# First slab on its own, its transfers ahead of the others, a fourth bank for slab 3, products of zeros at the start

## What is computed

```python
def rms_norm(x, g):
    y = xf * lax.rsqrt(jnp.mean(xf * xf, axis=-1, keepdims=True) + EPS)
    return (y * g.astype(jnp.float32)).astype(x.dtype)

for l in range(DEPTH):
    h = rms_norm(x, norm_mix_g[l])
    proj = h @ w_in[l]
    pa, pb, pc, pg = jnp.split(proj, GROUP_POINTS, axis=-1)
    oa = rwkv7_time_mix(pa, ...)      # decay, a and g come from the first 256 columns of pa
    ob = stick_breaking_attention(pb)
    oc = differential_attention(pc, ...)
    merged = ga * (oa @ w_branch_a[l]) + gb * (ob @ w_branch_b[l]) + gc * (oc @ w_branch_c[l])
    x = x + merged @ w_out[l]
    x = x + conv_ffn(rms_norm(x, norm_ffn_g[l]), ...)
```

## Time and profile before

| | us |
|---|---|
| median of 3 runs | 1148.99 |
| lowest, highest | 1147.91, 1149.82 |
| the profiled execution, its own time | 1146.43 |
| its span | 1144.5 |

### The profile page before, as it was taken

One profiled execution on the slowest core, in us unless ns is written; L12 is line 12 of the kernel. 1 busy time (PEld: TensorE's weight loads), 2 busy tenths in 40 slices (PEclk: granted clock), 3 DMA queues, 4 the chain that ended last, 5 costly groups with the idle time before them and its releaser, 6 DMA issues.

```text
span 1144.5 us, 26139 instructions
## 1 busy us (share of the span) xinstructions
PE 1089.9 (95%) x10100; PEld 1029.7 (90%) x10100; DVE 832.5 (73%) x1429; ACT 595.8 (52%) x884; POOL 2.5 (0%) x8
## 2 busy tenths in 40 slices
PE   6999999899999999999999999998999999999997
PEld 6998878789889999999999888877998899999996
DVE  5598586475768788778868975946657777877886
ACT  5861221555565655555578403026565656555556
POOL 0000000000000000000000000000000000000000
PEclk9999999999999999999999999999999999999999
DMA  7352321234435465665633413122453455556553
GB/s 277 110 168 93 94 92 57 74 129 149 150 119 193 132 217 168 189 188 173 187 128 129 149 61 108 58 92 73 135 172 130 144 179 163 187 178 190 182 173 125
DMA packets 46048, 163.47 MB, mean 143 GB/s; under 512 B 5552, under 2 KB 5728, under 8 KB 45968
## 3 DMA queue, kind: packets, MB, share of 16 engines
q1 hardware_dynamic: 45072, 160.88, 43.7%
q10 hardware_dynamic: 720, 1.14, 0.3%
q0 software_dynamic: 176, 0.29, 0.1%
HBM read 161.24 MB, written 1.05 MB: 142 GB/s over the span
## 4 chain that ended last, share of the span: by engine, by line
PE 72%; DVE 16%; ACT 6%; issue 5%; DMA 1%; DVEq 0%; ACTq 0%; SPq 0%
PE psum L441 71%; DVE sb_lo L1171 4%; ACT sb_rw L839 2%; ACT sb_inv L839 2%; ACT sb_hi L839 1%; DVE sb_inv L1379 1%; DVE sb_rw L1254 1%; DVE sb_inv L1387 1%; DVE sb_yf L1401 1%; DVE sb_small L1456 1%; DMA sb_raw<-w_stream 1%; DVE sb_rw L1239 0%; DVE sb_rw L1312 0%; DVE sb_inv L1369 0%; ACT sb_rs L839 0%
## 5 line engine op out<-in xcount | busy, mean ns | idle before, releaser
L441 PE MATMUL psum<-sb_hh,sb_hi 128*128 128x256 f32 x1568 | 457.5, 292 | 19.5 <-DVE sb_hl L1178 9.5
L441 PE MATMUL psum<-sb_hl,sb_hi 128*128 128x256 f32 x1568 | 446.6, 285 | 0.0
L441 PE MATMUL psum<-sb_hh,sb_lo 128*128 128x256 f32 x1568 | 446.3, 285 | 0.0
L839 ACT ACTIVATE sb_hi<-sb_raw 128x1024 fp32r<-128x1024 f32 (+1 forms) x301 | 313.2, 1046 | 248.3 <-PE psum L441 240.5
L1171 DVE TENSOR_TENSOR sb_lo<-sb_raw,sb_hi 128x1024 fp32r<-128x1024 f32 x297 | 362.4, 1221 | 100.2 <-ACT sb_hi L839 98.2
L441 PEld LDWEIGHTS psum<-sb_hh,sb_hi 128*128 128x128 f32 x1568 | 303.4, 194 | 29.1 <-issue 23.9
L441 PEld LDWEIGHTS psum<-sb_hl,sb_hi 128*128 128x128 f32 x1568 | 303.8, 194 | 2.0 <-issue 1.9
L441 PEld LDWEIGHTS psum<-sb_hh,sb_lo 128*128 128x128 f32 x1568 | 303.6, 194 | 0.0
L441 PE MATMUL psum<-sb_oh,sb_hi 128*128 128x256 f32 x672 | 192.4, 286 | 7.9 <-DVE sb_ol L1502 4.7
L441 PE MATMUL psum<-sb_ol,sb_hi 128*128 128x256 f32 x672 | 190.1, 283 | 0.0
L441 PE MATMUL psum<-sb_oh,sb_lo 128*128 128x256 f32 x672 | 190.1, 283 | 0.0
(11 more groups left out here) (166 smaller groups left out, 1027.6 us busy)
## 6 DMA issues: line engine op xcount, KB each, us to landing
sb_raw<-w_stream SPq DMA_DIRECT2D x298, 512.0 KB, 3.8
sb_pm<-mix_par ACTq DMA_DIRECT2D x2, 512.5 KB, 3.6
sb_raw<-w_stream SPq DMA_DIRECT2D x4, 256.0 KB, 6.1
sb_x<-x_t SPq DMA_DIRECT2D x4, 256.0 KB, 6.7
y_t<-sb_rw SPq DMA_DIRECT2D x4, 256.0 KB, 2.3
sb_cf<-const_f SPq DMA_DIRECT2D x1, 739.0 KB, 8.9
sb_pm<-mix_par SPq DMA_DIRECT2D x1, 512.5 KB, 10.4
sb_pf<-ffn_par POOLq DMA_DIRECT2D x3, 92.0 KB, 2.2
```

Of the source, the lines that this page charges most:

```text
L441: return pe.matmul(out, lhsT, rhs, start=start, stop=stop, skip_group_check=True)
L839: return act.activation(out, in_, func, scale=scale, bias=bias, **kw)
```

## The change

The outputs of the dense slabs get a table of banks: m = 0 to 3 go to banks 0, 1, 2 and 5, later ones go round banks 0 to 2; output 3 waits for none, output 4 for output 0, and so on, in both layers. "up" in addition waits until output 3 has been emptied, since it writes bank 5 too. In the first layer slab 0 is done alone (`first_slab`) and slab 1 as an ordinary slab; in the second layer the two stay woven. SP's first transfers are the halves of slab 0 with x tiles 0 to 3 between and behind them, then x tiles 4 to 7 in one, slabs 1 and 2 whole. ACT and DVE split slab 0 and x first, then slabs 1 and 2 whole. POOL's two loads wait until all eight tiles of x have been split. DVE first sets a 128 x 256 piece of `XSQ` to zero, and PE multiplies it with itself five times, in fp32, into bank 7; ACT's squares wait for that.

```diff
+BANK = [0, 1, 2, 5] + [(m - 4) % 3 for m in range(4, len(OUTS))]
+BEFORE = {m: max(p for p in range(m) if BANK[p] == BANK[m]) for m in range(4, len(OUTS))}
...
+X_PART = [slice(0, 2), slice(2, 4), slice(4, 8)]
...
-                sp.dma_start(x[:, 2 * b:2 * b + 2, :], x_t[:, 2 * b:2 * b + 2, :]).then_inc(x_in[b], 16)
-            for s in range(2):
-                sp.dma_start(raw[:, s, HALF[0]], w_in[s, :, HALF[0]]).then_inc(first_in[s], 16)
-                load_x(s)
-            for s in range(2):
-                sp.dma_start(raw[:, s, HALF[1]], w_in[s, :, HALF[1]]).then_inc(raw_in[s], 16)
-                load_x(2 + s)
-            sp.dma_start(raw[:, 2], w_in[2]).then_inc(raw_in[2], 16)
+                k = X_PART[b]
+                sp.dma_start(x[:, k, :], x_t[:, k, :]).then_inc(x_in[b], 16)
+            sp.dma_start(raw[:, 0, HALF[0]], w_in[0, :, HALF[0]]).then_inc(first_in, 16)
+            load_x(0)
+            sp.dma_start(raw[:, 0, HALF[1]], w_in[0, :, HALF[1]]).then_inc(raw_in[0], 16)
+            load_x(1)
+            load_x(2)
+            for s in (1, 2):
+                sp.dma_start(raw[:, s], w_in[s]).then_inc(raw_in[s], 16)
...
+            pool.wait_ge(split_l, KT)
...
-                    if m >= 3 and (n == 0 or m not in OUT_OF[n - 1]):
-                        pe.wait_ge(*n_out(l, m - 3))
+                    if m in BEFORE and m not in OUT_OF[n - 1]:
+                        pe.wait_ge(*n_out(l, BEFORE[m]))
...
+            def first_slab():
+                pe.wait_ge(first_lo, 1)
+                for k in range(KT):
+                    if k == KT // 2:
+                        pe.wait_ge(lo_done, 1)
+                    pe.wait_ge(split_l, k + 1)
+                    cols = slice(k * P, (k + 1) * P)
+                    last = split_mm(bank[0][:, 0:T], (hi[:, 0, cols], lo[:, 0, cols]), (hh[:, k, :], hl[:, k, :]),
+                                    k == 0, k == KT - 1)
+                last.then_inc(slab_done, 1)
...
+                    pe.wait_ge(*n_out(l, 3))
...
+            pe.wait_ge(zeros_set, 1)
+            for n in range(5):
+                last = mm(bank[7][:, 0:T], XSQ[:, 0, 0:P], XSQ[:, 0, :], n == 0, n == 4)
+            last.then_inc(zeros_used, 1)
...
-                            if l == 0 and b % 2 == 0:
-                                first_hi_of(b // 2)
-                                act.wait_ge(x_in[b], 16)
+                                if b < 2:
+                                    first_hi_of(b)
+                                if b < 3:
+                                    act.wait_ge(x_in[b], 16)
-                            split(2, 2, None, 16)
+                            for n in range(1, AHEAD):
+                                split(n, n, None, 16)
+                            act.wait_ge(zeros_used, 1)
...
-                            for t in range(4 * half, 4 * half + 4):
+                            for t in range(2, KT) if half else range(2):
-                        split(2, 2, None, None)
+                        for n in range(1, AHEAD):
+                            split(n, n, None, None)
...
+            dve.memset(XSQ[:, 0, :], 0.0).then_inc(zeros_set, 1)
```

More of the change, by code:

```diff
@@ L334, in hybrid_blocks @@
         const_in, fin_loaded = sem("const_in"), sem("fin_loaded")
-        x_in = [sem(f"x_in{b}") for b in range(4)]
-        first_in = [sem(f"first_half_in{s}") for s in range(2)]
+        x_in = [sem(f"x_in{b}") for b in range(3)]
+        first_in = sem("first_half_in")
         first_hi, first_lo = sem("first_half_hi"), sem("first_half_lo")
@@ L476, in dense @@
                             k, cols = 2 * i + k2, slice(k2 * BW, (k2 + 1) * BW)
-                            last = split_mm(bank[m % 3][:, :], (hh[:, k, tok], hl[:, k, tok]),
+                            last = split_mm(bank[BANK[m]][:, :], (hh[:, k, tok], hl[:, k, tok]),
                                             (hi[:, s, cols], lo[:, s, cols]), k == 0, k == KT - 1)
@@ L483, in dense @@
                             cols = slice(k * 2 * P + u * P, k * 2 * P + (u + 1) * P)
[L484 removed]
+                            last = split_mm(bank[BANK[m]][:, u * T:(u + 1) * T], (hi[:, s, cols], lo[:, s, cols]),
                                             (oh[:, b * BT + k, :], ol[:, b * BT + k, :]), u == 0 and k == 0,
@@ L493, in dense @@
                         cols = slice(k * P, (k + 1) * P)
-                        last = split_mm(bank[m % 3][:, 0:T], (hi[:, s, cols], lo[:, s, cols]),
+                        last = split_mm(bank[BANK[m]][:, 0:T], (hi[:, s, cols], lo[:, s, cols]),
                                         (src[0][:, k, :], src[1][:, k, :]), k == 0, k == KT - 1)
@@ L500, in two_slabs @@
             def two_slabs(slab, s0_, tiles):
[L502 to L505, removed]
+                pe.wait_ge(lo_done, slab + 2)
                 for k in range(KT):
-                    if slab == 0 and k == KT // 2:
-                        pe.wait_ge(lo_done, 2)
                     pe.wait_ge(split_l, tiles + k + 1)
@@ L533, in step @@
                 if kind == "D" and s[1] == 0:
-                    two_slabs(l * SLABS, 0, l * 2 * KT)
-                elif kind == "D" and s[1] > 1:
+                    if l:
+                        two_slabs(l * SLABS, 0, l * 2 * KT)
+                    else:
+                        first_slab()
+                elif kind == "D" and (s[1] > 1 or l == 0):
                     dense(l, s[1])
@@ L870, in empty @@
                     for tt, m in enumerate(OUT_OF[n]):
-                        do((vb if kind == "Bv" else vc)[:, tt, :], bank[m % 3][:, :], ACT.Copy,
+                        do((vb if kind == "Bv" else vc)[:, tt, :], bank[BANK[m]][:, :], ACT.Copy,
                            scale=rs[:, T + tt:T + tt + 1]).then_inc(emptied["act"], 1)
@@ L1086, in first_hi_of @@
             def first_hi_of(half):
-                for s in range(2):
-                    act.wait_ge((raw_in if half else first_in)[s], 16)
-                    do(hi[:, s, HALF[half]], raw[:, s, HALF[half]], ACT.Copy).then_inc(hi_done if half else first_hi, 1)
+                act.wait_ge(raw_in[0] if half else first_in, 16)
+                do(hi[:, 0, HALF[half]], raw[:, 0, HALF[half]], ACT.Copy).then_inc(hi_done if half else first_hi, 1)
                 if half == 0:
@@ L1209, in empty @@
             def empty(l, n):
-                kind, b = DENSE[n][0], bank[OUT_OF[n][0] % 3]
+                kind, b = DENSE[n][0], bank[BANK[OUT_OF[n][0]]]
                 if n == A_SLABS:
@@ L1505, in first_lo_of @@
             def first_lo_of(half):
-                for s in range(2):
-                    if half:
-                        dve.wait_ge(hi_done, s + 1)
-                    else:
-                        dve.wait_ge(first_hi, s + 1)
-                    cols = HALF[half]
-                    tt(lo[:, s, cols], raw[:, s, cols], hi[:, s, cols].bitcast(F32), ALU.subtract)\
-                        .then_inc(lo_done if half else first_lo, 1)
+                cols = HALF[half]
+                dve.wait_ge(hi_done if half else first_hi, 1)
+                tt(lo[:, 0, cols], raw[:, 0, cols], hi[:, 0, cols].bitcast(F32), ALU.subtract)\
+                    .then_inc(lo_done if half else first_lo, 1)
             def add_down(l, b):
```

5 lines of the change are left out of this document (3 added, 2 removed).

## The result

| | us |
|---|---|
| median after, 5 runs | 1142.01 (1140.27 to 1142.97) |
| median before, 5 runs | 1147.91 (1146.06 to 1149.82) |
| ratio, 95% interval | 0.9948 (0.9931 to 0.9965) |
| profiled execution after, its own time and span | 1142.97, 1141.3 |

The change is 5.9 us faster, against 5.2 forecast (1143.8, range 1140.9 to 1147.2). The time itself is 1.8 us under the forecast one: 0.7 is gain, and 1.1 comes from the kernel before, whose median is 1147.91 here and was 1148.99 in the three runs that the forecast started from.

What follows compares the result with a forecast made beforehand. PE was busy 1089.9 of 1144.5 us, so only its idle and slow time could be won: 1.6 (start) + 1.8 + 1.8 (layers) = 5.2 us, 1148.99 to 1143.8; own range 1142.4 to 1145.2, 8-in-10 range 1140.9 to 1147.2.

Steps and rivals of the forecast that it cites:

- The start: Program start to first norm: earlier x and slab 1, PE at the upper clock level in slabs 1 and 2; 1.6 us.
- second limit: ACT's first norm operation stands behind slab 5's split: slab 5 lands at 19.9, norm from 21.0, gain 1.5 us.
- signs of being wrong: Norm-to-sigmoids distance on ACT above 13, slab 1 after 14, or PE at 0.20 us a product in slabs 1 and 2.
- The waits inside slab 0: Slab 0 waits for x; expected upper clock level anyway, though by the skill's rule the start would be worth 0.3 us.
- rival (c): PE at the lower clock level when slab 1 starts, for one stretch: 3.9 us gained, 1145.1; chance 0.06.
- The zeros: Five fp32 products ahead of slab 0, over by about 5.7, before x arrives at 6.5: cost 0.
- The bank: Slab 3 behind the norm starts without waiting for DVE; ACT's sigmoids start 1.8 us earlier in each layer.
- (a): PE's whole loss comes back, at the start and 2.7 us a layer: 7.6 us gained, 1141.4; chance 0.14.
- (b): The start gives nothing or costs, by old transfer pace and one half-clock stretch: 2.8 us gained, 1146.2; chance 0.18.
- (d): The banks give nothing because later waits of ACT and DVE absorb it: 1.6 us alone, 1147.4; chance 0.06.
- (e): Slower: PE waits for slab 1 until 14.6, lower clock level through slab 3: 2.4 us lost, 1151.4; chance 0.04.
- The disturbance is moved and not removed: By the skill's rule, delaying POOL's loads only shifts the slow transfers, leaving the start the 1.5 us of the second limit.

Runs made afterwards that it cites:

- the second profile: The changed kernel, unaltered, timed and profiled again beside the other kernels: 1140.82 us, ratio 0.9948 to the kernel before.
- the run with E 3 first: The changed kernel with DVE's emptying of slab 3's bank moved ahead of slab 6's lo part, both layers: 1140.09 us, ratio 0.9949.

## Why the prediction was right

The sign, the size and the path are right: 5.2 us forecast, 5.9 measured twice. The time, 1142.01, is in the range and just under the narrower one that was given for the forecast itself (1142.4 to 1145.2). Both layers' terms are shown. The term of the start is not, and that the whole came so near is in part luck. By its steps:

**The start, 1.6 us.** Its numbers on transfers and splits held: first product at 6.5 (6.94), all x on ACT at 10.6 (11.0), slab 1 from 12.9 (13.26), slab 5 at 19.9 (19.68). Slab 5 came near from a reading that was off: the rows from 8 to 10 us are 307 and 363 GB/s, 335 on average and not 320, and 335 would have put it at 20.1. And 1.6 is more than the 1.5 to which the prediction's own second limit holds the term. What failed is the level of the clock: I had PE at the upper level in slabs 1 and 2, from "PE is active enough in slab 0", and the norm on PE at 18.5. It began at 20.04; the clock was half from 8.5 to 15.4. That is one of the prediction's own signs of being wrong, PE at 0.20 us a product, and it held for the first nine of slab 1. In the second profile, with slab 1 at the upper level, the norm on PE was at 19.11. The term came out at 0.65 in the one profile and 1.57 in the other. The second limit, slab 5 ahead of the norm on ACT, lay at 21.0 as worked out and hid a part of the error: ACT's norm came 0.9 us late in the one (21.88) and in time in the other (20.96). Without that limit the term would have been 2.2, and 1.5 too large in the one. Nor is 22.53 a firm mark: with nothing of the start changed the norm came at 21.91, and from there the two are worth 0.03 and 0.95 us. By the times the start is worth 1.9 us alone (2.2 by the ratio, 0.8 to 3.4) and 1.4 on top of the bank. So the rows put the term between 0 and 1.6 and the times between 0.8 and 3.4, and no run fixes it closer.

**The waits inside slab 0.** The rows show the fall at 8.5, 9.6, 8.6, 8.8 and 11.2 in five executions with five products of zeros and waits of 0.3 to 2.5 us for x, and none in the two with the waits filled. By the Trainium skill (TensorE: Matmul & The Clock Gate, "HAM oscillation — how this bites in real kernels") waits for data between groups of products bring the array back to half rate. The trace agrees, with shorter waits than the 3 to 5 us of the kernel told of there. I had given it too little: rival (c) had a chance of 0.06, and in four of the five executions slab 1 did begin at the lower level. The price was smaller than (c)'s 1.3 us, because the clock rose again 1.1 to 2.1 us into slab 1; in the fifth it was up at 13.06, ahead of slab 1.

**The zeros, cost 0.** Right: they end at 5.6 and slab 0 waits until 6.94. But as placed they gain nothing that was measured.

**The bank, 1.8 us a layer.** Measured 1.98 (13.93 to 11.95 or 11.94) with the order on DVE as it was, in both layers. The tanh moved by 0.57 (0.6 forecast). The mechanism was right, ACT and DVE cap what PE gains, and the run with E 3 first shows the cap: it gave 0.86 more. What I had not seen is how the term is made up: without a fall of the clock in the kernel before it would have been 0.5. I wrote that the clock behind the norm changes the gain hardly at all. For a fall in the changed kernel that stays untested, since no trace has one there; for the fall in the kernel before it is wrong, as that fall is three quarters of the term.

**The rivals.** (a) is refuted by the rows: PE's 2.7 us a layer don't come back, 2.0 do. The times alone would allow its 7.6 us (the intervals reach 7.9 and 7.7). (b), 2.8 us in all, is refuted by them: by their intervals the gain is at least 4.0. (d) is refuted by the layers' rows: what ACT had gained at 33.83, 2.6 us, was still there at 68.89 (71.54 before). (e) didn't come.

**POOL's loads.** I took the slow rates from 3 to 7 us for theirs. Half right: without them the rates rise from 5 us on. "The disturbance is moved and not removed", which I had drawn from the Trainium skill (DMA: Bandwidth & Descriptors, "Queues, rings and completion order"), is not what the rates show: a dip of about a tenth from 16 to 17 us is what is left of it, and slab 5 comes 0.8 us earlier with the loads delayed.

## What to carry to other kernels

Where PE waits for one bank whose emptying hangs on a norm, look at the granted clock behind the wait before sizing it: here the wait was 1.4 us, its removal gave 0.5, and the fall that often followed it 1.5. To keep the clock up at the start of a program, try filling the waits inside the first group of products too: five products of zeros ahead of it alone were undone by the next waits, twelve in both places were not. And compare executions with their falls listed: one fall more or less is 1.3 to 1.6 us, as much as a whole edit. A page's PEclk row is too coarse for that, since it shows 9 throughout for the kernel before, which has three falls; the stretches show them.

## What the runs showed of the hardware

Falls of the granted clock last 3.4 or 6.8 us here. They come at a few places: inside slab 0, behind PE's 1.41 us wait for a bank, behind the 64x64 instructions on sb_yf and sb_inv (11 falls at 40 such places in ten profiles), and at PE's 2.04 us wait ahead of a 128x512 product (3 falls at 20). Which of them has one changes from execution to execution of one kernel: 8.5 and 117.8 in one of the changed kernel, 9.6 and 214.4 in the other. A fall of 3.4 us cost 1.3 us behind the norm (19 products where 30 fit), 1.6 at 117.8 and 1.5 at 745.6. The pause of 1.41 us ahead of slab 3 brought a fall in three of the four layers where a profile has it, and in none of the sixteen without it.

The rate of transfers drops to 88 to 137 GB/s from 4 to 5 us in all eight executions with the new order of SP's transfers, with GpSimd's loads at once or delayed, and to 172 and 177 in the two with the old order; what causes that was not tried. GpSimd's two loads (4 and 92 KB) made the transfers that were issued beside them at the start 1.3 us later; issued behind the split of x they left a dip to 360 to 389 GB/s from 16 to 17 us, where the three executions with early loads have 402 to 421.
